# Retention outputs with tokens as rows, and four batches' memory scores side by side, in a hybrid decoder step

## The reference

```python
def retention(s0, q, k, v):          # per head; chunks of 128 (the prompt), of 8 (a sample)
    ...
        scores = jnp.einsum('bihd,bjhd->bhij', qc, kc) * decay_mask
        o = (jnp.einsum('bhij,bjhe->bihe', scores, vc)
             + jnp.einsum('bihd,bhde->bihe', qc * q_decay[None, :, :, None], s))
        s = (chunk_decay[None, :, None, None] * s
             + jnp.einsum('bjhd,bjhe->bhde', kc * k_decay[None, :, :, None], vc))
...
def head_groupnorm(o):
    mu = jnp.mean(o, axis=-1, keepdims=True)
    var = jnp.mean(jnp.square(o - mu), axis=-1, keepdims=True)
    return (o - mu) * lax.rsqrt(var + EPS)

def mem_attend(q, k, v):
    s = jnp.einsum('bthd,bmhd->bhtm', q, k).astype(F32) * (MEM_HD ** -0.5)
    p = jax.nn.softmax(s, axis=-1).astype(v.dtype)
    return jnp.einsum('bhtm,bmhd->bthd', p, v)
...
            mix = (head_groupnorm(o).reshape(b, t, RET_W) * jax.nn.silu(g)).astype(h.dtype)
```

## Time and profile before

| | us |
|---|---|
| median of 3 runs (1691.4 to 1693.68) | 1692.91 |
| the profiled execution | 1694.59 |
| its span, first to last instruction | 1692.8 |
| TensorE busy in it | 1588.5 |
| DVE busy | 831.6 |
| ACT busy | 563.0 |
| mean granted clock of TensorE, share of full | 0.971 |

### The profile page before, as it was taken

The page is one execution under the profiler, slowest core; times in us unless marked ns, Lnnn a source line. Parts: engine busy times, 40 slices in busy tenths (PEclk is TensorE's granted clock), DMA queues, the critical chain, the costliest instruction groups (busy, mean ns, idle before and its releaser), DMA issues.

```text
span 1692.8 us, 28971 instructions
## 1 busy us (share of the span) xinstructions
PE 1588.5 (94%) x11509; PEld 1467.0 (87%) x11509; DVE 831.6 (49%) x1238; ACT 563.0 (33%) x882; POOL 50.9 (3%) x77
## 2 busy tenths in 40 slices
PE   3889999878999999999989689999999999999998
PEld 3868999868999999999988556766799999999998
DVE  5845666654543433424576645665454334333344
ACT  4412223333331322313432115554343223132234
POOL 1120000001000000000000000000000000000000
PEclk8999999979999999999999888999999999999999
DMA  6532332203222232222323221543222223322221
GB/s 195 173 107 84 90 89 77 77 27 106 76 86 83 82 88 76 86 86 77 84 83 107 61 84 34 148 133 84 73 76 76 88 76 89 86 77 85 86 80 63
DMA packets 229463, 149.61 MB, mean 88 GB/s; under 512 B 11137, under 2 KB 222482, under 8 KB 229362
## 3 DMA queue, kind: packets, MB, share of 16 engines
q1 hardware_dynamic: 218802, 122.57, 25.1%
q0 software_dynamic: 6112, 20.54, 3.9%
q10 hardware_dynamic: 4448, 5.11, 0.9%
HBM read 140.52 MB, written 7.68 MB: 88 GB/s over the span
## 4 chain that ended last, share of the span: by engine, by line
PE 83%; DVE 11%; ACT 4%; issue 1%; DMA 1%; ACTq 0%; DVEq 0%; SPq 0%
PE ps L572 63%; PE ps L1055 3%; PE ps L1013 2%; PE ps L1082 2%; DVE wl L1534 2%; PE ps L996 1%; ACT wh L1163 1%; PE ps L923 1%; PE ps L700 1%; PE ps L958 1%; PE ps L959 1%; DVE t L1839 1%; PE ps L777 1%; PE ps L781 1%; DVE rstd L1553 1%
## 5 line engine op out<-in xcount | busy, mean ns | idle before, releaser
L572 PE MATMUL ps<-xh,wh 128*128 128x288 f32 x1542 | 338.2, 301 | 9.0 <-DVE wl L1534 9.0
L572 PE MATMUL ps<-mh,wh 128*128 128x288 f32 (+1 forms) x1424 | 324.9, 297 | 17.2 <-DVE wl L1534 15.9
L572 PE MATMUL ps<-xl,wh 128*128 128x288 f32 x1542 | 330.8, 296 | 0.0
L572 PE MATMUL ps<-xh,wl 128*128 128x288 f32 x1542 | 330.7, 296 | 0.0
L572 PE MATMUL ps<-ml,wh 128*128 128x288 f32 (+1 forms) x1424 | 322.5, 295 | 0.0
L572 PE MATMUL ps<-mh,wl 128*128 128x288 f32 (+1 forms) x1424 | 322.2, 295 | 0.0
L1163 ACT ACTIVATE wh<-raw 128x1024 fp32r<-128x1024 f32 (+1 forms) x195 | 202.2, 1037 | 277.9 <-PE ps L572 260.1
L1534 DVE TENSOR_TENSOR wl<-raw,wh 128x1024 fp32r<-128x1024 f32 (+1 forms) x195 | 232.9, 1194 | 88.8 <-ACT wh L1163 87.8
L572 PEld LDWEIGHTS ps<-xh,wh 128*128 128x128 f32 x1542 | 250.7, 191 | 17.0 <-DVE wl L1534 10.3
L572 PEld LDWEIGHTS ps<-mh,wh 128*128 128x128 f32 x1424 | 236.9, 190 | 20.1 <-DVE wl L1534 16.6
L572 PEld LDWEIGHTS ps<-xl,wh 128*128 128x128 f32 x1542 | 250.0, 190 | 0.0
(11 more groups left out here) (298 smaller groups left out, 1409.5 us busy)
## 6 DMA issues: line engine op xcount, KB each, us to landing
raw<-in_w_up SPq DMA_DIRECT2D x64, 512.0 KB, 4.0
raw<-in_w_down SPq DMA_DIRECT2D x64, 512.0 KB, 3.6
pages<-in_cache_mla SPq DMA_DIRECT2D x128, 160.0 KB, 2.2
raw<-in_a_w_in SPq DMA_DIRECT2D x26, 512.0 KB, 3.9
memkc<-in_cache_mem_k POOLq DMA_DIRECT2D x16, 256.0 KB, 3.8
memvc<-in_cache_mem_v POOLq DMA_DIRECT2D x16, 256.0 KB, 4.4
raw<-in_a_w_out SPq DMA_DIRECT2D x8, 512.0 KB, 4.1
raw<-in_b_w_out SPq DMA_DIRECT2D x8, 512.0 KB, 4.5
```

The costliest lines, as they stand in the source:

```text
L572: last = mm(ps[:, 2 * (m % 2) + c, 0:n], w[:, s, kk, :], x(kk, col, n), start=(kk == 0 and nth == 0), stop=(kk == k - 1 and nth == 2))
```

## The change

Retention outputs are made with tokens on the partitions: `ret_out` swaps its operands and writes bank 4, and the samples' outputs come as 64 rows of bank 7. Mean and variance of each row come from `bn_stats` and `bn_aggr` on DVE, the root from ACT in one operation, then DVE takes the mean off and scales (`onorm`), and `ret_back` turns the result back to features on partitions for gate and split. `ret_cent`, `ret_sums`, `ret_norm`, `cent`, `osb` and ACT's copies are gone. The state update multiplies 32 rows (four batches) at a time with four blocks of `vexp` instead of 64 rows with eight; `qexp` and the mask tiles shrink with it.

`mem_samples` is split into functions, placed anew in each engine's list. Keys get four slots, are evicted by ACT, and the scores of four batches are made together, their matmuls alternating over four groups of 32 columns. In layer 0 the second group's turn and back stand inside tiles. The buffers `rcn` and `kcT` move, and ACT waits for older output transfers ahead of `rcn`.

The diff, cut to its core (TensorE first, then ACT, then DVE; layer 1's lists follow the same pattern as TensorE's, shown once):

```diff
-                def scores(b):
-                    bq, g = b % 4, b // 4
-                    pe.wait_ge(ms_kT, NB * layer + b + 1)
-                    if b == 0:
-                        pe.wait_ge(ms_q, layer + 1)
-                    elif bq == 0:
-                        pe.wait_ge(ms_exp, 2 * layer + g)
-                    for j in range(2):
-                        last = mm(ps[32 * bq:32 * bq + 32, bank + 2, 0:NMEM], qb[:, j, b, :], kcT[:, b % 2, j, :],
...
+            def sample_scores(layer, g):
+
+                G, mb = 2 * layer + g, mem[layer]
+                pe.wait_ge(ms_kT, NB * layer + 4 * g + 4)
+                pe.wait_ge(*((ms_exp, G) if g else (ms_q, layer + 1)))
+                for j in range(2):
+                    for bq in range(4):
+                        last = mm(ps[32 * bq:32 * bq + 32, 6, 0:NMEM], mb["qblk"][:, j, 4 * g + bq, :], mb["kcT"][bq][:, j, :],
                                   start=(j == 0), stop=(j == 1))
-                    if bq == 3:
-                        last.then_inc(ms_sc, 1)
...
+                last.then_inc(ms_sc, 1)
...
                 for half in range(2):
-                    mm(ps[:, 5 + half, :], krs[:, :], vexp[:, 4 * half:4 * half + 4, :].rearrange("p b e -> p (b e)"), start=True, stop=True)
+                    rows = slice(32 * half, 32 * half + 32)
+                    mm(ps[:, 5 + half, :], krs[rows, :], vexp[rows, :, :].rearrange("p b e -> p (b e)"), start=True, stop=True)
                 pe.wait_ge(s0_in, 16 * (h + 1))
-                mm(ps[:, 7, 0:NS], vrs[:, :], aTs[:, :], start=True, stop=False)
-                for b in range(NB):
-                    last = mm(ps[:, 7, 0:NS], s0[:, b, :], qexp[:, b, :], start=False, stop=(b == NB - 1))
+                for half in range(2):
+                    rows = slice(32 * half, 32 * half + 32)
+                    mm(ps[rows, 7, 0:P], aTs[:, rows], vrs[:, :], start=True, stop=False)
+                for b in range(NB // 2):
+                    for half in range(2):
+                        rows = slice(32 * half, 32 * half + 32)
+                        last = mm(ps[rows, 7, 0:P], qexp[:, 4 * half + b, :], s0[:, 4 * half + b, :], start=False, stop=(b == NB // 2 - 1))
                 last.then_inc(r_kv, 1)
 
             def ret_out(h):
-                pe.wait_ge(r_os, h + 1)
                 pe.wait_ge(r_state, h + 1)
                 for n in range(RT):
-                    last = mm(ps[:, 7, P * n:P * n + P], vrow[:, n, :], aT[:, n, :], start=True, stop=(n == 0))
+                    last = mm(ps[:, 4, P * n:P * n + P], aT[:, n, :], vrow[:, n, :], start=True, stop=(n == 0))
                     if n:
-                        last = mm(ps[:, 7, P * n:P * n + P], st[:, n - 1, :], qd[:, P * n:P * n + P], start=False, stop=True)
+                        last = mm(ps[:, 4, P * n:P * n + P], qd[:, P * n:P * n + P], st[:, n - 1, :], start=False, stop=True)
                 last.then_inc(r_o, 1)
 
-            def ret_cent(h):
-
-                pe.wait_ge(r_osb, h + 1)
-                for c in range(2):
-                    last = mm(ps[:, 5 + c, 0:HALF], cent[:, :], osb[:, HALF * c:HALF * c + HALF], start=True, stop=True)
-                last.then_inc(r_cent, 1)
-
-            def ret_sums(h):
-
-                pe.wait_ge(r_sq, h + 1)
-                for n in range(RT + 1):
-                    rows = P if n < RT else NS
-                    last = mm(ps[0:rows, 4, n:n + 64], ss[:, P * n:P * n + rows], ones[:, 0:64], start=True, stop=True)
-                last.then_inc(r_var, 1)
-
-            def ret_norm(h):
-
-                pe.wait_ge(r_diag, h + 1)
-                for c in range(2):
-                    last = mm(ps[:, (4, 7)[c], P:P + HALF], ones[:, :], sq[:, HALF * c:HALF * c + HALF], start=True, stop=True)
-                last.then_inc(r_inv, 1)
+            def ret_back(h):
+
+                pe.wait_ge(r_norm, h + 1)
+                for n in range(RT):
+                    pe.transpose(ps[:, 5, P * n:P * n + P], onorm[:, n, :], ident[:, :])
+                pe.transpose(ps[:, 6, 0:NS], onorm[0:NS, RT, :], ident[0:NS, 0:NS]).then_inc(r_back, 1)
 
             def z_tile(h, part, middle=None):
                 for ks in (range(KD // 2), range(KD // 2, KD)):
@@ -818,16 +779,40 @@
                     if middle and 0 in ks:
                         middle(h - 1)
 
-            mem_samples(0, lambda n: z_tile(0, Z_SIDES[n]) if n in Z_SIDES else None)
+            def first_turn(h):
+                sample_turn(0, 1)
+
+            def first_back(h):
+                sample_back(0, 1)
+
+            sample_keys(0, 0)
+            sample_keys(0, 1)
+            z_tile(0, 0)
+            sample_keys(0, 2)
+            sample_keys(0, 3)
+            sample_scores(0, 0)
+            z_tile(0, 1)
+            sample_keys(0, 4)
+            sample_keys(0, 5)
+            sample_turn(0, 0)
+            sample_keys(0, 6)
+            sample_keys(0, 7)
+            sample_values(0, 0)
+            z_tile(0, 2)
+            sample_scores(0, 1)
+            sample_back(0, 0)
+            z_tile(0, 3, first_turn)
+            sample_values(0, 1)
             for h in range(1, H_RET):
-                for part, (middle, end) in enumerate(((None, ret_rows), (None, ret_kv), (ret_out, ret_cent), (ret_sums, ret_norm))):
+                for part, (middle, end) in enumerate(((first_back if h == 1 else None, ret_rows), (None, ret_kv), (ret_out, None), (ret_back, None))):
                     z_tile(h, part, middle)
                     if (h, part) == (H_RET - 1, 3):
                         mem_step(0, 0)
                         mem_step(0, 1)
-                    end(h - 1)
-
-            last_head = {2: ret_rows, 4: ret_kv, 6: ret_out, 7: ret_cent, 9: ret_sums, 11: ret_norm}
+                    if end:
+                        end(h - 1)
+
+            last_head = {2: ret_rows, 4: ret_kv, 6: ret_out, 9: ret_back}
...
+            sample_keys(1, 0)
+            sample_keys(1, 1)
+            qb_tile(0)
+            sample_keys(1, 2)
+            sample_keys(1, 3)
+            qb_tile(1)
+            sample_scores(1, 0)
+            qb_tile(2)
+            sample_keys(1, 4)
+            sample_keys(1, 5)
+            sample_turn(1, 0)
+            qb_tile(3)
+            sample_keys(1, 6)
+            sample_keys(1, 7)
+            sample_values(1, 0)
+            qb_tile(4)
+            sample_scores(1, 1)
+            sample_back(1, 0)
+            qb_tile(5)
+            qb_tile(6)
+            sample_turn(1, 1)
+            qb_tile(7)
+            sample_values(1, 1)
+            qb_tile(8)
+            sample_back(1, 1)
...
+            def sample_exp(layer, g):
+                G, mb = 2 * layer + g, mem[layer]
+                act.wait_ge(ms_max, G + 1)
+                do(f(mb["ES"][:, :], ps[:, 6, 0:NMEM], ACT.Exp, bias=vec[:, 33:34], scale=MEM_SCALE,
+                     accum_out=vec[:, 34:35]), C[ms_exp])
+
+            def sample_turn(layer, g):
...
             def ret_kv(h):
-                act.wait_ge(r_kv, h + 1)
-                do(f(osb[:, SEQ:ROWS], ps[:, 7, 0:NS], ACT.Copy), C[r_os])
+                pass
 
             def ret_out(h):
-                act.wait_ge(r_o, h + 1)
-                do(f(osb[:, 0:SEQ], ps[:, 7, :], ACT.Copy), C[r_osb])
-
-            def ret_cent(h):
-                act.wait_ge(r_cent, h + 1)
-                do(f(halves(ss[:, :]), ps[:, 5:7, 0:HALF], ACT.Square), C[r_sq])
-
-            def ret_sums(h):
 
                 act.wait_ge(r_var, h + 1)
-                do(f(vec[:, 40:40 + RT], ps[:, 4, 0:RT], ACT.Sqrt, bias=EPS, scale=1.0 / P))
-                do(f(vec[0:NS, 40 + RT:41 + RT], ps[0:NS, 4, RT:RT + 1], ACT.Sqrt, bias=EPS, scale=1.0 / P), C[r_std])
-
-            def ret_norm(h):
+                do(f(gn[:, 0:RT + 1], gn[:, 6 * (RT + 1) + 1:8 * (RT + 1):2], ACT.Sqrt, bias=EPS), C[r_std])
+
+            def ret_back(h):
                 act.wait_ge(r_mix, h + 1)
                 do(f(mh[:, h, :], t1[:, :], ACT.Copy), C[r_hi])
...
-                do(tt(qexp[:, :, :], qd[:, SEQ:ROWS].unsqueeze(1).to_broadcast([P, NB, NS]), blkq[:, :, :], ALU.mult))
-                do(tt(vexp[:, :, :], vrs[:, :].unsqueeze(1).to_broadcast([NS, NB, P]),
-                      blkv[:, :].unsqueeze(2).to_broadcast([NS, NB, P]), ALU.mult), C[r_dve])
+                for half in range(2):
+                    c = SEQ + 32 * half
+                    do(tt(qexp[:, 4 * half:4 * half + 4, :], qd[:, c:c + 32].unsqueeze(1).to_broadcast([P, NB // 2, NS // 2]), blkq[:, :, :], ALU.mult))
+                do(tt(vexp[:, :, :], vrs[:, :].unsqueeze(1).to_broadcast([NS, NB // 2, P]),
+                      blkv[:, :].unsqueeze(2).to_broadcast([NS, NB // 2, P]), ALU.mult), C[r_dve])
...
             def ret_out(h):
-                pass
-
-            def ret_cent(h):
-                pass
-
-            def ret_sums(h):
-
+
+                def rows(n):
```

(63 more changed lines are left out.)

316 lines of the change are left out of this document (142 added, 174 removed).

## The result

| | before | after |
|---|---|---|
| median of 4 runs, us | 1693.3 (1691.4 to 1693.86) | 1652.72 (1650.64 to 1654.08) |
| the profiled execution, us | 1694.59 | 1651.49 |
| its span, us | 1692.8 | 1649.7 |
| TensorE busy, us | 1588.5 | 1547.9 |
| mean granted clock | 0.971 | 0.970 |

The ratio of the times is 0.9761, 95% interval 0.9744 to 0.9778: 40.6 us less by the medians and 43.1 by the spans of the two profiles. Forecast were 1647 us with a range of 1636 to 1663. The page of the changed kernel, part 1 (busy us, share of the span, instructions), against the earlier trace rows: TensorE has lost 40.6 us of work and keeps its share; DVE has lost 3.7, ACT gained 2.6.

What follows compares the result with a forecast made beforehand. TensorE, busy 94% of the span, was taken to bound the kernel. Savings of 13.5 + 22.5 + 0 + 10.5 = 46.5 us from 1694.6 give 1648.1 (1646.4 against the median); forecast 1647, 8-in-10 range 1636 to 1663.

Steps and rivals of the forecast that it cites:

- Layer 0, samples: Samples' memory attention of layer 0, woven with head 0's projection tiles: 13.5 us saved, bounds 11 to 14.5.
- a slow stretch: In layer 0's samples' stretch, an allowance of 1.0 us for one tile running slowly after a wait.
- Heads: Retention in heads 1 to 5: 4.7 us saved per head, 22.5 in all, bounds 11 to 25.
- the row pair: Two state matmuls in `ret_kv`, 32 rows each, expected side by side: 0.91 us instead of 1.82.
- the old wait for `vexp`: TensorE's wait in heads after the first, expected to go: 1.15 us saved per head.
- Statistics chain: Row statistics after `ret_out`: 6.5 us against two half tiles of 6.4, so 0.3 to 0.5 of wait.
- The rival's ten operations: Late statistics: ten small operations at 0.45 us make the chain 8.6, wait 2.3 per head; 1658.6 us, chance 0.15.
- Last head: Last head woven with the prompt's memory attention: gains and losses cancel, 0 us, bounds -4 to +4.
- Layer 1: Samples' memory of layer 1 woven with nine query tiles: 47.8 against 58.4 us, 10.5 saved, bounds 7 to 12.
- Row groups: Rival: groups don't overlap in `ret_kv`; row groups alone 1652.5 us, both kinds 1658; chance 0.13.
- The clock in the heads: Rival: lower clock in heads 1 to 5, tiles 12.8 instead of 6.4 us, up to 1775; chance 0.03.
- The woven stretches: Rival: they hide the gain, last head -4 and layer 1 only 7 saved; 1654.5 us, chance 0.09.

Runs made afterwards that it cites:

- the run of the samples' half alone: The changed kernel with retention as in the kernel before, keeping only the new memory attention of the samples: 1668.42 us.
- the one with the longer state pair: The changed kernel with the samples' state update back over 64 rows and eight blocks of `vexp`: 1660.23 us.
- the one with the spread rotaries: The changed kernel with layer 1's three rotary query tiles third, fifth and seventh instead of last: 1653.74 us.
- The kernel with all three edits: The changed kernel with turns back later, last head's statistics behind the prompt's last maximum and exponentials, and layer 1's rotary tiles spread: 1641.96 us.
- the one with the later turns: The changed kernel with `ret_back` of heads 0 to 3 moved to the middle of the next head's first tile: 1651.27 us.

## Why the prediction came out right

- **Layer 0, samples** (13.5 forecast, 15.0). Scores 1.0, wait 0.94, keys and values as priced. The 1.0 us for a slow stretch was not needed, as the clock is 1.00 in all 35.91 us. The reason given for the price, one column group for both matmuls of a batch, was only half of it: full-width turns between batches kept the groups apart, and the order of the loops does nothing. The loads of the states were hidden: `ret_kv` of head 1 doesn't wait.
- **Heads** (22.5 forecast, 19.6). This is the step that was mis-sized. Four head periods save 17.7 in all (156.5 before, 138.8 after), 4.4 each and not 4.7: the row pair 1.06 for 0.91, `ret_kv` 3.38 for 3.2, the turns 0.8 and their wait 0.6, the old wait for `vexp` 1.03 on the average for 1.15. The fifth head saves 2.1, where I had 3.5: its broadcast lies behind the end of this stretch, and I had counted it here and again in the last head's. The first tile takes 0.2 more for the samples' last back.
- **Statistics chain** (6.5 forecast with its hand-overs; 6.8 from 147.82 to 154.62, 7.0 from the end of `ret_out` at 147.71 to the turns at 154.67). `bn_stats` 0.32 each for 0.29, `bn_aggr` 0.21 for 0.155, the normalising operation 0.44 for 0.34, the root's detour 1.68 for 1.6. The wait of 0.58 to 0.75 is what this leaves over two half tiles (6.4), and it goes when the root goes. The rival's ten operations at 0.45 add up to 8.8 and not 8.6.
- **Last head** (0 forecast, 1.0 lost). Named in the prediction with its two causes, but too small: the time from the end of `ret_out` to the output projection is 5.2 longer and not 2.6. TensorE idles 9.65 us in it where it idled 4.06: 6.79 for the queue on DVE, 0.75 for the second load, 2.00 in front of the projection. Up to the end of `ret_out` the stretch gained 4.2. Luck has a part in how this stretch reads: in both profiles compared here the last head had the better clock. From the last `ret_kv` to the end of `ret_out` the new retention took 17.7 us, but 20.6 to 20.9 in seven of the runs; the old one took 20.3, but 24.0 in the run of the samples' half alone.
- **Layer 1** (10.5 forecast, 11.1; the stretch 47.3 for 47.8). DVE binds at the end: TensorE waits 5.82 for `ml` at 930.76.
- **Rivals.** Row groups do overlap, and changing between the shapes in `ret_kv` costs little: the next full-width tile starts 1.0 us after the first of the sixteen records of L758, which two column groups share, where the earlier trace rows have 1.81 for sixteen full-width ones of 64 columns. With 128 columns, as here, the fourteen full-width records of `ret_out` take 1.48 us (145.99 to 147.47), sixteen would take 1.69. Half of either is 0.85 to 0.9, so 0.1 to 0.15 is left for every change there, by this estimate. The clock in the heads stayed at 1.00. The statistics were late by 0.6, not 2.3. The woven stretches did not hide the gain, save for 1.0.
- **What is left over**: 1.6 us in the code between the stretches, unchanged by the edit. From the output projection to layer 1's first keys the profiled executions of these kernels scatter from 523.4 to 527.8 us (524.3 before, 525.2 after), and behind layer 1's stretch from 715.8 to 719.3 (718.7 before, 718.9 after), so a difference of that size can't be put down to the change. What exactly moves it was not tried.

The forecast's sum was 3.4 above the one read from the two profiles, 2.9 of it in the heads. The forecast time is 5.7 us below the median; the rest comes from the profiled executions, of which the old kernel's lay 1.3 above its median and the new one's 1.2 below.

## What to carry to other kernels

Matmuls that use a part of the array are cheap only next to one another: bring those of several batches together, and keep full-width work such as turns out from between them; four batches of scores then cost what one did (1.0 us). When a step's chain moves to an engine that was idle, check the whole queue there, and place it behind the work that TensorE needs first: in the last head the same operations cost 5 us more in front of a maximum than behind it. And when stretches are summed, list for each instruction in which stretch it lies, so that none is counted twice.

## What the runs showed of the hardware that was not expected

- The order in which four column groups are issued doesn't matter: 1.0 us for eight fp32 matmuls of 256 columns, alternating or by group. One full-width matmul between two groups' pairs makes each pair 0.98 us.
- Two fp32 matmuls of 512 columns over 32 rows each, in two row groups and two banks, take 1.06 us side by side; over 64 rows, both in the same rows, 1.91.
- The granted clock of a woven stretch with waits differs from execution to execution for the same code. From the last `ret_kv` to the end of `ret_out`, 17.6 to 18.0 us in three profiles of the new retention and 20.6 to 20.9 in seven, 19.8 in the one with the longer state pair. The changed kernel and the one with the spread rotaries came to it alike: in both TensorE was busy 1.67 us from 313 to 318, and then the one was granted 0.74 and the other 0.50 over the 20 us shown above. They differ in when the clock fell: the changed kernel was granted 0.83 from 314.38 to 316.38 and was back at 1.00 from 324.38 to 328.38, the other still had 1.00 from 314.65 to 316.65 and then 0.50 from 318.65 to 340.65. The kernel with all three edits went as the changed kernel did, the one with the later turns as the other. What decides when the clock goes from one level to the other (1.2 and 2.4 GHz) isn't settled; it makes single profiles of this kernel unfit to judge an edit under 3 us.
